# Gate products of the last two token tiles by Strassen's method in a hybrid layer kernel

## What is computed

```python
    gate = jax.nn.sigmoid((_rmsnorm(h, norm_ple) @ ple_gate_w + ple_gate_b).astype(jnp.float32))
    h = h + (gate * (p @ ple_proj_w).astype(jnp.float32)).astype(h.dtype)
...
return _rmsnorm(h, norm_final), ...
```

## Time and profile before

| | |
|---|---|
| median of 3 runs | 537.75 us (537.75 to 538.51) |
| the profiled execution, its own time | 537.61 us |
| its span (first to last instruction) | 536.0 us |
| mean granted TensorE clock | 0.986 |
| busy: PE, DVE, ACT, POOL | 93%, 40%, 29%, 21% |

### The profile page before, as it was taken

One profiled execution on the slowest core, in us unless ns is written; L12 is line 12 of the kernel. 1 busy time (PEld: TensorE's weight loads), 2 busy tenths in 40 slices (PEclk: granted clock), 3 DMA queues, 4 the chain that ended last, 5 costly groups with the idle time before them and its releaser, 6 DMA issues.

```text
span 536.0 us, 7862 instructions
## 1 busy us (share of the span) xinstructions
PE 500.9 (93%) x3132; PEld 303.7 (57%) x3132; DVE 216.8 (40%) x520; ACT 154.5 (29%) x318; POOL 111.6 (21%) x169
## 2 busy tenths in 40 slices
PE   5999999999999998899999999988888989999994
PEld 4888886888545444555555555544544543444443
DVE  2187696523035556762222222212111111569345
ACT  1436263112615021212222222221121224455113
POOL 0300058994201002101111111110111122031001
PEclk9999999999999999999999999998988999999998
DMA  8993000503469805999999999999999997940012
GB/s 312 390 332 114 1 1 6 230 11 79 157 264 395 364 18 182 407 414 416 414 415 416 414 417 415 414 420 413 414 421 412 417 411 257 358 190 39 2 40 79
DMA packets 41576, 145.70 MB, mean 272 GB/s; under 512 B 14620, under 2 KB 15260, under 8 KB 32420
## 3 DMA queue, kind: packets, MB, share of 16 engines
q1 hardware_dynamic: 33888, 131.69, 62.4%
q0 software_dynamic: 5152, 8.71, 4.4%
q10 hardware_dynamic: 2500, 4.79, 2.4%
HBM read 141.24 MB, written 15.24 MB: 292 GB/s over the span
## 4 chain that ended last, share of the span: by engine, by line
PE 70%; DMA 12%; DVE 7%; SPq 7%; ACT 1%; issue 1%; ACTq 0%; POOLq 0%; POOL 0%; DVEq 0%
PE PS L1062 14%; PE PS L821 10%; PE PS L1176 10%; PE PS L636 10%; DMA mem<-in_exp_w_up 9%; PE PS L1083 7%; PE PS L607 5%; PE PS L596 4%; SPq L500 2%; SPq L494 2%; DMA mem<-in_w_a 2%; SPq L496 2%; DVE mem L1740 1%; DMA mem<-choice_rows 1%; PE PS L1069 1%
## 5 line engine op out<-in xcount | busy, mean ns | idle before, releaser
L1062 PE MATMUL PS<-mem 128*64 128x256 f32 x512 | 122.3, 394 | 13.1 <-DMA mem<-in_exp_w_up 12.9
L1063 PE MATMUL PS<-mem 128*64 128x256 f32 x512 | 122.4, 394 | 0.0
L1062 PEld LDWEIGHTS PS<-mem 128*64 128x64 f32 x512 | 69.8, 141 | 49.8 <-DMA mem<-in_exp_w_up 10.5
L636 PE MATMUL PS<-mem 128*128 128x260 f32 x320 | 73.2, 386 | 0.0
L1063 PEld LDWEIGHTS PS<-mem 128*64 128x64 f32 x512 | 69.8, 141 | 0.0
L636 PEld LDWEIGHTS PS<-mem 128*128 128x128 f32 x320 | 60.0, 190 | 10.4 <-issue 1.5
L2055 DVE TENSOR_TENSOR mem<-PS,mem 64x256 f32<-64x256 f32 x32 | 13.7, 427 | 128.5 <-ACT mem L1384 128.3
L1083 PE MATMUL PS<-mem 128*64 128x512 f32 x256 | 62.0, 605 | 1.1 <-ACT mem L1390 0.7
L821 PE MATMUL PS<-mem 128*128 128x512 f32 x128 | 57.0, 597 | 0.0
L1176 PE MATMUL PS<-mem 128*128 128x512 f32 (+1 forms) x144 | 56.0, 547 | 0.0
L1384 ACT ACTIVATE mem<-PS 64x256 f32<-64x256 f32 x32 | 12.0, 375 | 110.7 <-PE PS L1063 110.7
(11 more groups left out here) (294 smaller groups left out, 547.7 us busy)
## 6 DMA issues: line engine op xcount, KB each, us to landing
mem<-in_exp_w_down SPq DMA_DIRECT2D x32, 1024.0 KB, 23.7
mem<-in_exp_w_gate SPq DMA_DIRECT2D x32, 1024.0 KB, 21.4
mem<-in_exp_w_up SPq DMA_DIRECT2D x32, 1024.0 KB, 23.6
mem<-in_w_out SPq DMA_DIRECT2D x2, 2048.0 KB, 7.7
mem<-in_ple_gate_w SPq DMA_DIRECT2D x2, 2048.0 KB, 16.8
mem<-choice_rows SPq DMA_DIRECT2D x4, 1024.0 KB, 13.6
mem<-in_x_prompt SPq DMA_DIRECT2D x4, 512.0 KB, 13.9
mem<-in_w_v SPq DMA_DIRECT2D x1, 2048.0 KB, 24.6
```

The source lines that it names most:

```text
L636: ins = pe.matmul(PS[b + h][:, 0:HALF], w[:, k, :], aT[:, k, h * HALF:(h + 1) * HALF], start=(k == 0), stop=(k == KT - 1))
L1062: pe.matmul(PS[0][0:S, 0:FF], rows_k, gu[slot][:, k, :], start=(k == 0), stop=(k == KT - 1))
L1063: ins = pe.matmul(PS[1][S:2 * S, 0:FF], rows_k, gu[slot][:, KT + k, :], start=(k == 0), stop=(k == KT - 1))
```

## The change

The gate products of positions 3 and 4 (tiles 2 and 3, 256 rows by 1024 by 1024) are computed together as a product of 2x2 blocks. A row block is 128 tokens by 512, a weight block 512x512. The eight block products are replaced by seven, in Winograd's form of Strassen's method. It needs:

- four sums of weight blocks (`w_sum`, each 128 partitions x 2048 elements in SBUF), made by GpSimd in one instruction each, with both operands in SBUF. They stand between the `inverse_root`s in GpSimd's queue: the first behind the root of position 2, before those of 3 and 4; the second behind `root_h3(0)`; the third behind `root_h3(1)`; the fourth behind the third and a wait for the second half of `gates(2)`, whose weights it overwrites.
- four sums of turned row blocks (`sum_rows`, 128x512), made by VectorE behind `take_h2_rows(4)`.
- sums of products (`first_sums`, `second_sums`, `last_gate`), made by VectorE, 12 instructions where five `gate_sum`s stood.
- rows that are scaled before they are turned, since the block products mix tokens: ScalarE writes `hn` (two instructions of 128x1024) behind `square_h3(0, 1)`, and `h2_rows(3)` and `h2_rows(4)` wait for them.

`h2_rows(4)` moves from between the halves of `gates(3)` into the second half of `gates(2)`. The order of the pieces at the end, of their stores and of ScalarE's queue is rewritten. Some semaphores outside the tail are merged in pairs, with the waits on them at the same places.

```diff
+LAST = [(0, 512), (512, 1024)], [(512, 1024), (0, 256), (256, 512)]
+LAST_TURN = {(3, 0): 8, (3, 1): 9, (4, 0): 7, (4, 1): 10, (4, 2): 11}
+P_11, P_S2, P_S3, P_S1, P_12, P_S4, P_22 = range(7, 14)
+
+def pieces(i):
+
+    return LAST[i - 3] if i >= 3 else [(0, 512), (512, 1024)]
+
+
+def turn(i, j):
+
+    return LAST_TURN.get((i, j), 2 * i + j + 1)
+
+        hn = at(R_row, 2, D)
+        uT_last = [uTr[:, 1, :], at(R_gu + 2 * GU + 7 * D, D)]
+        w_sum = [at(R_v, 4, 512), at(R_aT, 4, 512), at(R_aT + 2 * D, 4, 512), w_ple[1][:, 0:4, :]]
+        u_sum = [Yg[3][:, 1, 512:D], Yg[2][:, 1, 0:512], Yg[2][:, 1, 512:D], Yg[3][:, 1, 0:512]]
+        d_bple = at(R_dt, 512)
...
                 t = TAIL[i]
                 R = ROWS[t]
                 for half in range(2):
-                    pe.wait_ge(s_f_h2, 2 * i + half + 1)
+                    if i >= 3:
+                        pe.wait_ge(s_f_hn, i - 2)
+                    else:
+                        pe.wait_ge(s_f_h2, 2 * i + half + 1)
                     if i >= 1:
                         pe.wait_ge(s_f_vT, 2 * i - 1 + half)
+                    rows = hn[:, i - 3, :] if i >= 3 else h1[0:R, t, :]
                     for q in range(4):
                         k = 4 * half + q
-                        ins = transpose(PS[6 + half][:, q * P:q * P + R], h1[0:R, t, k * P:(k + 1) * P], R)
+                        ins = transpose(PS[6 + half][:, q * P:q * P + R], rows[:, k * P:(k + 1) * P], R)
                     ins.then_inc(s_f_T, 1)
...
+                        if h == 0 and k % 4 == 0:
+                            pe.wait_ge(s_f_vT, 2 * i + k // 4 + 1)
+                        if i == 2 and h == 1 and k == 4:
+                            h2_rows(4)
+                        ins = pe.matmul(PS[h][:, :] if i == 2 else PS[2 * (i % 2) + h][:, :], uTr[:, i % 2, k * P:(k + 1) * P],
+                                        w_ple[h][:, k, :], start=(k == 0), stop=(k == KT - 1))
+            def product(bank, rows, w):
+
+                for k in range(4):
+                    ins = pe.matmul(bank, rows[:, k * P:(k + 1) * P], w[:, k, :], start=(k == 0), stop=(k == 3))
+                ins.then_inc(s_f_g, 1)
+
+            def last_gates():
+                t1, t2, t3, t4 = w_sum
+                s1, s2, s3, s4 = u_sum
+                a11, a12, a22 = uT_last[0][:, 0:512], uT_last[0][:, 512:D], uT_last[1][:, 512:D]
+                pe.wait_ge(s_f_gb, 4)
+                pe.wait_ge(s_f_vT, 8)
+                product(PS[2][:, :], a11, w_ple[0][:, 0:4, :])
+                pe.wait_ge(s_f_wsum, 2)
+                pe.wait_ge(s_f_vT, 12)
+                product(PS[3][:, :], s2, t2)
+                pe.wait_ge(s_f_wsum, 3)
+                pe.wait_ge(s_f_vT, 13)
+                pe.wait_ge(s_f_gb, 5)
+                product(PS[0][:, :], s3, t3)
+                pe.wait_ge(s_f_gb, 6)
+                product(PS[1][:, :], s1, t1)
+                product(PS[5][:, :], a12, w_ple[0][:, 4:KT, :])
+                pe.wait_ge(s_f_gb, 7)
+                pe.wait_ge(s_f_vT, 14)
+                product(PS[3][:, :], s4, w_ple[1][:, 4:KT, :])
+                pe.wait_ge(s_f_wsum, 4)
+                for q in range(2):
+                    product(PS[4 - 2 * q][:, 0:256], a22, t4[:, :, q * 256:(q + 1) * 256])
...
+            for i in (3, 4):
+                act.wait_ge(s_inverse_root, 2 * NT + i + 1)
+                A(hn[:, i - 3, :], h1[:, TAIL[i], :], ACT.Copy, scale=rstd[:, 10 + TAIL[i]:11 + TAIL[i]]).then_inc(s_f_hn, 1)
...
+            square_h3(2, 0)
+            square_h3(2, 1)
+            sigmoid(4, 0)
+            sigmoid(3, 0)
+            square_h3(4, 0)
+            square_h3(3, 0)
+            sigmoid(3, 1)
+            square_h3(3, 1)
+            sigmoid(4, 1)
...
+            def sum_w(j, a, b):
+
+                pool.tensor_tensor(w_sum[j], a, b, ALU.subtract).then_inc(s_f_wsum, 1)
+
+            b11, b21, b12, b22 = [w_ple[h][:, k:k + 4, :] for h in range(2) for k in (0, 4)]
+            root_h2(0)
+            root_h2(1)
+            root_h2(2)
+            pool.wait_ge(s_pp_done, len(PP_PARTS))
+            for h in range(2):
+                pool.wait_ge(ld_wple[h], 16)
+            sum_w(0, b12, b11)
+            root_h2(3)
+            root_h2(4)
+            root_h3(0)
+            pool.wait_ge(s_f_wsum, 1)
+            sum_w(1, b22, w_sum[0])
+            root_h3(1)
+            sum_w(2, b22, b12)
+            pool.wait_ge(s_f_g, 6)
+            pool.wait_ge(s_f_wsum, 3)
+            sum_w(3, b21, w_sum[1])
+            for i in range(2, NT):
+                root_h3(i)
...
+            def sum_rows():
+
+                s1, s2, s3, s4 = u_sum
+                (a11, a12), (a21, a22) = [(u[:, 0:512], u[:, 512:D]) for u in uT_last]
+                dve.wait_ge(s_f_vT, 10)
+                last(tt(s1, a21, a22, ALU.add), s_f_vT, 11)
+                last(tt(s2, s1, a11, ALU.subtract), s_f_vT, 12)
+                tt(s3, a11, a21, ALU.subtract).then_inc(s_f_vT, 1)
+                tt(s4, a12, s2, ALU.subtract).then_inc(s_f_vT, 1)
...
+            g_11, g_12, g_21, g_22 = [Yg[t][:, 0, h * 512:(h + 1) * 512] for t in (2, 3) for h in range(2)]
+
+            def first_sums():
+
+                step(tt(d_bple, bple[:, 512:D], bple[:, 0:512], ALU.subtract))
+                dve.wait_ge(s_f_g, P_11)
+                step(tt(g_11, PS[2][:, :], bple[:, 0:512], ALU.add))
+                dve.wait_ge(s_f_g, P_S2)
+                step(tt(g_21, PS[3][:, :], g_11, ALU.add))
+                step(tt(g_12, g_21, d_bple, ALU.add))
+
+            def second_sums():
+
+                dve.wait_ge(s_f_g, P_S3)
+                tt(g_21, PS[0][:, :], g_21, ALU.add)
+                step(tt(g_22, PS[0][:, :], g_12, ALU.add))
+                dve.wait_ge(s_f_g, P_S1)
+                step(tt(g_12, PS[1][:, :], g_12, ALU.add))
+
+            def last_gate(product, gate, bank, other):
+
+                dve.wait_ge(s_f_g, product)
+                tt(gate, bank[:, 0:gate.shape[1]], other, ALU.add).then_inc(s_f_gb, 1)
...
             finish(1)
+            take_h2_rows(4)
+            sum_rows()
             gate_sum(2, 1)
             apply_gate(2, 0)
-            gate_sum(3, 0)
-            take_h2_rows(4)
             apply_gate(2, 1)
-            gate_sum(3, 1)
+            first_sums()
+            finish(2)
+            second_sums()
+            last_gate(P_S1, g_22, PS[1], g_22)
+            apply_gate(4, 0)
+            last_gate(P_12, g_11, PS[5], g_11)
+            t = TAIL[NT - 1]
+            tt(yout[:, t, 512:D], h1[:, t, 512:D], bfin[:, 512:D], ALU.mult)
             apply_gate(3, 0)
-            finish(2)
+            last_gate(P_S4, g_12, PS[3], g_12)
             apply_gate(3, 1)
-            gate_sum(4, 0)
-            apply_gate(4, 0)
             finish(3)
-            t = TAIL[NT - 1]
-            gate_sum(4, 1)
-            tt(yout[:, t, 0:512], h1[:, t, 0:512], bfin[:, 0:512], ALU.mult)
-            gate_sum(4, 2)
+            last_gate(P_22, g_21[:, 0:256], PS[4], g_21[:, 0:256])
+            last_gate(P_22 + 1, g_21[:, 256:512], PS[2], g_21[:, 256:512])
             apply_gate(4, 1)
             apply_gate(4, 2)
-            step(tt(yout[:, t, 512:1024], h1[:, t, 512:1024], bfin[:, 512:1024], ALU.mult))
+            step(tt(yout[:, t, 0:512], h1[:, t, 0:512], bfin[:, 0:512], ALU.mult))
             dve.wait_ge(s_inverse_root, 4 * NT)
```

More of the change, by code:

```diff
@@ L358, in build @@
         s_acs_ready = sem("s_acs_ready")
-        s_tri_done = sem("s_tri_done")
+        s_tri_G_done = sem("s_tri_G_done")
         s_tri_out = sem("s_tri_out")
@@ L367, in build @@
         s_Rh_out = sem("s_Rh_out")
-        s_BC_done = sem("s_BC_done")
+        s_BC_eE_done = sem("s_BC_eE_done")
         s_BC_out = sem("s_BC_out")
@@ L418, in build @@
         s_f_ya = sem("s_f_ya")
+        s_f_wsum = sem("s_f_wsum")
+        s_f_hn = sem("s_f_hn")
         s_f_vT = sem("s_f_vT")
@@ L583, in _ @@
             t = TAIL[NT - 1]
-            for h in (1, 0):
-                if h == 0:
+            for h in (0, 1):
+                if h == 1:
                     sp.wait_ge(s_f_ya, 1)
@@ L1169, in gates @@
                         pe.wait_ge(s_pp_out, len(PP_PARTS) - 3 + h)
[L1170 to L1178, removed]
+                    for k in range(KT):
+                        if h == 0 and k % 4 == 0:
[4 more added lines that the diff above has]
+                                        w_ple[h][:, k, :], start=(k == 0), stop=(k == KT - 1))
@@ L1187, in _ @@
             gate_samples()
-            for i in range(2, NT):
-                gates(i)
+            gates(2)
+            last_gates()
         @block.scalar
@@ L1291, in _ @@
             out(J_V + 2)
-            act.wait_ge(s_BC_done, 1)
+            act.wait_ge(s_BC_eE_done, 1)
             for q in range(4):
                 A(BC[:, q, :], PS[4 + q][:, :], ACT.Copy).then_inc(s_BC_out, 1)
-            act.wait_ge(s_eE_done, 1)
```

(28 more changed lines are left out.)

25 lines of the change are left out of this document (12 added, 13 removed).

## The result

The changed kernel takes 549.81 us (median of 6 runs, 548.59 to 550.95), the kernel before 538.21 us (6 runs, 537.75 to 539.19). The ratio is 1.0207, 95% interval 1.019 to 1.0223: slower by 11.6 us. The profiled execution took 548.59 us, its span is 546.9 us.

What follows compares the result with a forecast made beforehand. TensorE was taken to bound the tail, with VectorE only 0.9 us ahead. Saved product -0.6, stalls +9.5 and slow clock +1.7 gave +10.6 us on the profiled 537.61: 548.2 us, range 541.5 to 551.5.

Steps and rivals of the forecast that it cites:

- the 0.9 us of room: Near 484 us, VectorE's first half of `take_h2_rows(2)` is done 0.9 us before TensorE starts `gates(2)`, which needs it.
- What goes and what of it reaches the end: In TensorE's tail, one block product of eight goes, 3.44 us; behind `finish(3)` only 0.6 us of it arrives.
- The rival of the full product: At the end, the last gates don't queue behind `finish(3)`, so all 3.44 us are saved: 534.2 us, chance 0.05.
- Eleven more VectorE instructions, scaled copies, moved transposes at 0: In the tail, VectorE's extra 8 us fit its idle time, copies cost 0 to 0.5 us, transposes 0.87 in either place.
- Price of a sum: Each GpSimd weight sum of 2048 elements takes 4.1 us, the middle of 3.6 and 4.5.
- VectorE shut out to the end of the instruction: VectorE instructions with two SBUF operands wait until GpSimd's two-operand sum ends, 4.1 us a sum.
- The three stalls: TensorE waits for VectorE near 485, 499 and 510 us: 3.05, 3.4 and 3.05 us, 9.5 us in all.
- the same walk: Following the tail's queues sum by sum, at 4.1 us each, to find TensorE's waits: 9.5 us.
- The clock: TensorE's clock falls to half speed for 3.5 us, counting in full behind the third stall: 1.7 us, bounds 0 and 3.4.
- One stall less: Rival: one of TensorE's three tail stalls falls away, leaving 6.4 us of stalls: 543.4 to 545.1 us, chance 0.20.

Runs made afterwards that it cites:

- The last run: Changed kernel with weight sums made by ScalarE's negative copies and adding transfers, and `finish(3)` moved behind `apply_gate(4, 2)`: 536.1 us, ratio 0.9961 to the kernel before.

## Why the prediction was right, point by point

- **What bounds the kernel, and the 0.9 us of room.** Right. TensorE was the chain, and the first stall is VectorE's delay less that room: `take_h2_rows(2)` is 4.1 us late (487.51 against 483.44), TensorE was ready 0.2 us sooner, less 0.9 of room; 3.50 us measured.
- **What goes and what of it reaches the end.** Right to the tenth in the profiled executions: from TensorE's end to the end of the span it is 2.8 us more, so of 3.44 us 0.6 arrive; without the sums the tail is 0.6 us shorter. The medians can't show 0.6 us. The rival of the full product didn't come: the last gates stood behind `finish(3)`. The last run shows that this held 1.9 us of the 2.8.
- **Eleven more VectorE instructions, scaled copies, moved transposes at 0.** Right: ratio 1.000 without the sums.
- **Price of a sum.** Mis-sized: 4.1 us taken as the middle of 3.6 and 4.5, 4.50 to 4.68 measured. The middle of two rows was the poorer choice; the row with the higher price gave the right one. The Trainium skill (GPSIMD Engine Reference, 3.1, Elementwise) gives 4497 ns for 2048 elements. The trace agrees: three of the four sums took 4.50 to 4.52 us.
- **VectorE shut out to the end of the instruction.** Right for two operands, now seen at four times the length the rows had; each sum cost VectorE 3.8 to 4.2 us. With one operand VectorE was let in after 3.6 of 5.5 us. The Trainium skill's sentence on the whole instruction (SBUF — State Buffer, Who interferes with whom) agrees with the trace for two operands, and not for one.
- **The three stalls.** The places are right. 3.05, 3.4 and 3.05 us forecast, 3.50, 3.37 and 2.57 measured. With sums of 4.5 us the same walk gives about 3.5, 3.8 and 3.9. The second is smaller because two sums made VectorE 8.2 us late (502.30 against 494.14) and not 8.6, the third because the slow clock had already delayed TensorE.
- **The clock.** Half right. It fell as foreseen, but behind the second stall and not the third, and the 1.45 us there shortened the third stall. It was not free for that: the fourth sum overwrites the weights of these products, and its row shows 1.80 us of waiting for them, so part of the slow clock can have reached the end that way, by an estimate from this row at most 1.8 us; no run separates it. Against the forecast there are two errors that cancel: longer sums, +1.6 us, and no slow clock behind the third stall, -1.7. That the profiled execution lies only 0.4 us above the forecast is luck to that extent. The median lies 1.6 us above it. The clock may be why, but this is not shown, since only one of the executions has a trace: of the six, those with a mean granted clock of 0.985 and 0.986 took 548.7 and 548.6 us, those with 0.977 550.1 and 550.95, but 0.979 goes with 549.5 and 0.983 with 550.2.
- **One stall less.** The rival didn't come. The order it hung on went as in the walk: sum and `finish` 0.2 us apart, with the sum first.

## What to carry to other kernels

Before moving element work to GpSimd, look at what VectorE does at that time. Where its instructions read two operands from SBUF, the two engines took turns here, and a GpSimd instruction with two operands of 4.5 to 4.7 us cost VectorE up to 4.2, all that was left of it when VectorE's instruction came. It cost the kernel nothing where no engine on the chain soon needed what VectorE makes, and VectorE lost no time where it worked from PSUM. A product saved on TensorE in the last microseconds is worth only what VectorE's queue lets through: look for the instruction that waits for something else ahead of the last ones.

## What the runs showed of the hardware that was not expected

- A GpSimd instruction with one operand (a product with a constant) is no shorter than a subtraction of two: 5.36 to 5.50 us against 4.50 to 4.68 for 2048 elements. It let VectorE in about 1.9 us before its end.
- GpSimd instructions back to back don't always let a waiting VectorE instruction in between: in the first sum in quarters they took turns (1.64 to 1.77 us for VectorE's 0.75), in the third all four quarters passed ahead of it (5.77 us). What decides it was not tried.
- GpSimd waits for VectorE as well: its two one-column instructions took 0.69 and 0.88 us beside two-operand work on VectorE, and 0.19 and 0.55 without.
- The granted clock doesn't fall behind every idle time of 3.4 to 3.5 us: behind the first in one kernel (3.37 us idle), not in another (3.50).
- An adding transfer of 1 MB, issued by GpSimd in 1.3 us beside two-operand work on VectorE, landed in 8.6 us and slowed nothing that the tail waits for.
